# A two-block transformer kernel on one core: order of the linear-attention tail, its norm read out of PSUM, and one wait split in two

## The chip, the cores and the metric

The kernel runs on one core of one Trainium2 chip. The metric is the device time of one execution in microseconds. Before the change the median of three runs was 2160.75 us (2159.34 to 2163.74).

## The reference

Two transformer blocks, one after the other, on 512 tokens of width 1024. The change lies in the first block's gated linear attention (GLA): 4 heads, keys and queries 64 wide, values 128 wide, both directions.

```
q, k, v, g per head; cum = cumsum(g) within a chunk
o_inter = (q * exp(cum)) @ state                       # from the states between chunks
attn    = sum_d q_i k_j exp(cum_i - cum_j), masked     # within a chunk
o       = o_inter + attn @ v                           # both directions added
state   = exp(last) * state + (k * exp(last - cum)).T @ v
out     = rmsnorm(o, gla_norm_g) * silu(r)             # per head, over its 128 columns
mix     = concat([out, diff_attention_out]) @ w_out
x       = x + gate * mix                               # then norm2 and the feed-forward
```

Differential attention (`diff_tensor`, `diff_scalar`, `diff_vector`) runs just before the GLA and gives the other four of the eight 128-row pieces that `w_out` takes.

## The kernel before

Every activation lies transposed, feature on partitions and 512 tokens along the free dimension. A large product is made in three fp32r passes (high weight by high input, high by low, low by high; `three_passes`, L405), so each weight slot of 128 x 1024 is split: ScalarE rounds it to `w_hi` (`split_slots`, L418), GpSimd subtracts to `w_lo` (L1631). Slots come through a ring of four raw buffers, filled by SyncE in stream order; two pairs of split buffers are used by turns. Each engine has one program in a written order, and semaphores tie them. A PSUM bank is taken with `claim` (waits until the last user has freed it) and handed over with `full`.

The GLA is made in chunks of 128 tokens. Keys decayed to the chunk's edge (`key_decay`, `decayed_keys`) are turned (`keys_turned`, L1201 and L1206) and multiplied with the values to the states between chunks (L1228). Between these, TensorE computes the eight chunks `mixed_values_chunk(0..7)` of `w_out` for the differential half (12 matmuls of 512 columns each, 3 passes x 4 pieces). The attention within a chunk is made by levels: level 0 is the diagonal (`gla_level(pe, 0)`, `attention(0)`), and levels 1 to 7 halve the distance each time. For level `li`, VectorE writes four differences of running sums (`sums`, L1389 to L1392: two into `lk`, two into `lq`), ScalarE takes the exponentials of `lk` and `lq` (`level_decay`, L1291), GpSimd multiplies `lk` by the keys (L1429), VectorE `lq` by the queries (L1409), TensorE makes four banks of products (`gla_level`, L1190), banks 0 to 3 for even levels and 4 to 7 for odd, and VectorE (L1376; for levels 1 and 2 ScalarE, L1302) puts them into `attnT`. VectorE's order within turn `li` is: L1409 of `li`, `sums(li + 1)`, `attention(li - 1)`.

Then come the outputs: for each head 4 products of `attnT` with the values (L1247) and 8 of the states with the decayed queries `qe` (L1251) add up in banks 4 to 7. ScalarE copies each output to `og` (L1330) and squares it (L636), TensorE sums the squares over partitions (`head_sum`, L619), ScalarE takes the root (L641), VectorE the reciprocal (L663), TensorE spreads it (`head_spread`, L627), VectorE multiplies it in with the gain (L667) and then with the gate `rT` (L671), ScalarE rounds to `hh` (L652) and VectorE subtracts to `hl` (L657). The first weight slot of the next projection, `mix1`, is split by ScalarE just before it rounds the last head. `half_mixed_tensor` computes the projection, output chunk by output chunk (m = 0 to 7, 12 matmuls each), and `mixed_chunk` (L1488) adds each to the residual.

## Time and profile before

| what | value |
|---|---|
| median of 3 runs | 2160.75 us |
| the profiled execution | 2151.61 us, its span 2149.7 us |
| TensorE matmul busy | 2014.5 us, 94% |
| TensorE weight load busy | 1610.4 us, 75% |
| VectorE, ScalarE, GpSimd busy | 929.1, 739.3, 703.2 us |
| mean granted TensorE clock | 0.961 of full |
| the stretch that the diff touches | about 356 to 487 us of the span |

The profile covers one execution. A slice's or window's PEclk of 1.00 is a TensorE clock of 2.4 GHz, 0.50 is 1.2 GHz. Matmul rows are counted in parts (an fp32 product gives two rows). "Idle before" is the time for which the engine sat still ahead of an instruction, with what it waited for.

### The profile page before, as it was taken

The page shows a single profiled execution, that of the slowest core. Times are in us where ns is not written, and L with a number is a line of the kernel's source. Part 1 is how long each engine was busy: PE and PEld are TensorE (multiplying, and loading weights), DVE is VectorE, ACT ScalarE, POOL GpSimd, SP SyncE. Part 2 cuts the span into 40 slices and gives each one's busy share as a digit, 9 for nine tenths or more (in the row PEclk, how much of TensorE's full clock was granted, in tenths as well). Part 3 has the DMA queues.
Part 4 walks back from the last instruction along what each step waited for, and adds up shares of the span by engine and source line. Part 5 has one row for each costly group of instructions (what it writes and reads, how often), then busy time and mean ns, then how long its engine had stood idle before and what let it go on. Part 6 is the DMA issues. An engine that isn't in the chain of part 4 may idle for free.

```text
span 2149.7 us, 25842 instructions
## 1 busy us (share of the span) xinstructions
PE 2014.5 (94%) x10133; PEld 1610.4 (75%) x10136; DVE 929.1 (43%) x1363; ACT 739.3 (34%) x1202; POOL 703.2 (33%) x296
## 2 busy tenths in 40 slices
PE   5899988879999999999999999889989999999998
PEld 3787856667888888788888877756857777888886
DVE  2622587764344430444443334666775323222102
ACT  3433345433222221422222134536265333222211
POOL 0332100223344444334444423210401433444442
PEclk8999989879999999999999999899989999999999
DMA  8633210002344452334445522200200222232221
GB/s 330 205 130 101 94 56 14 21 11 98 126 142 144 154 195 90 99 125 147 146 151 183 184 70 84 69 30 21 90 29 30 89 79 88 98 98 98 90 96 59
DMA packets 60126, 223.61 MB, mean 104 GB/s; under 512 B 6800, under 2 KB 7056, under 8 KB 58256
## 3 DMA queue, kind: packets, MB, share of 16 engines
q1 hardware_dynamic: 59472, 220.13, 30.1%
q10 hardware_dynamic: 576, 2.43, 0.3%
q8 instruction: 51, 0.84, 0.2%
q14 instruction: 27, 0.22, 0.0%
HBM read 220.43 MB, written 2.10 MB: 104 GB/s over the span
## 4 chain that ended last, share of the span: by engine, by line
PE 85%; DVE 8%; ACT 3%; issue 2%; DMA 1%; SPq 0%; POOL 0%; DVEq 0%; ACTq 0%
PE ps L405 74%; PE ps L537 2%; DMA raw<-stream 1%; DVE t L601 1%; DVE hl L593 1%; PE ps L947 1%; PE ps L2014 1%; PE ps L2167 1%; PE ps L966 1%; DVE neg_max L1104 1%; PE ps L2176 1%; PE ps L1190 0%; ACT w_hi L418 0%; PE ps L2036 0%; DVE step L2297 0%
## 5 line engine op out<-in xcount | busy, mean ns | idle before, releaser
L1631 POOL TENSOR_TENSOR w_lo<-raw,w_hi 128x1024 fp32r<-128x1024 f32 x278 | 670.6, 2413 | 1369.0 <-ACT w_hi L418 765.4
L405 PE MATMUL ps<-hh,w_hi 128*128 128x512 f32 x1528 | 611.1, 400 | 34.3 <-DVE hl L593 17.9
L405 PE MATMUL ps<-hl,w_hi 128*128 128x512 f32 x1528 | 603.4, 395 | 0.0
L405 PE MATMUL ps<-hh,w_lo 128*128 128x512 f32 x1528 | 602.6, 394 | 0.0
L405 PEld LDWEIGHTS ps<-hh,w_hi 128*128 128x128 f32 x1528 | 291.2, 191 | 108.4 <-issue 26.1
L405 PEld LDWEIGHTS ps<-hh,w_lo 128*128 128x128 f32 x1528 | 291.5, 191 | 62.9
L405 PEld LDWEIGHTS ps<-hl,w_hi 128*128 128x128 f32 x1528 | 291.9, 191 | 59.4
L1604 ACT ACTIVATE w_hi<-raw 128x1024 fp32r<-128x1024 f32 x126 | 133.7, 1061 | 472.5 <-PE ps L405 472.5
L464 DVE SCALAR_TENSOR_TENSOR mod_raw<-mod_raw,cond_ada 128x1024 f32<-128x1024 f32 x72 | 116.2, 1615 | 249.7 <-DMA mod_raw<-late 249.7
L405 PE MATMUL ps<-act_hi,w_hi 128*128 (+1 forms) x528 | 209.3, 396 | 0.0
L405 PE MATMUL ps<-act_lo,w_hi 128*128 (+1 forms) x528 | 209.3, 396 | 0.0
L405 PE MATMUL ps<-act_hi,w_lo 128*128 (+1 forms) x528 | 209.3, 396 | 0.0
L1664 DVE TENSOR_TENSOR act_lo<-prod,act_hi 128x512 fp32r<-128x512 f32 x66 | 156.4, 2369 | 57.2 <-ACT act_hi L1609 57.2
L418 ACT ACTIVATE w_hi<-raw 128x1024 fp32r<-128x1024 f32 x92 | 96.9, 1055 | 186.7 <-PE ps L405 183.2
L1623 ACT ACTIVATE w_hi<-raw 128x1024 fp32r<-128x1024 f32 x60 | 63.6, 1061 | 267.6 <-PE ps L405 267.6
L1661 DVE TENSOR_TENSOR prod<-silu,ps 128x512 f32<-128x512 f32 x66 | 45.4, 688 | 216.9 <-PE ps L405 209.0
L405 PEld LDWEIGHTS ps<-act_hi,w_lo 128*128 128x128 f32 x528 | 99.4, 188 | 24.3
L405 PEld LDWEIGHTS ps<-act_lo,w_hi 128*128 128x128 f32 x528 | 99.4, 188 | 24.2
L405 PEld LDWEIGHTS ps<-act_hi,w_hi 128*128 128x128 f32 x528 | 99.4, 188 | 24.2
L464 DVE SCALAR_TENSOR_TENSOR raw<-raw,cond 128x1024 f32<-128x1024 f32 x32 | 47.5, 1499 | 66.5 <-DMA raw<-stream 61.5
L537 PE MATMUL ps<-cst,sq 128*128 128x128 f32 x456 | 63.1, 296 | 10.5 <-ACT sq L556 10.2
L537 PEld LDWEIGHTS ps<-cst,sq 128*128 128x128 f32 x456 | 60.6, 208 | 15.7 <-issue 8.4
(405 smaller groups left out, 2284.8 us busy)
## 6 DMA issues: line engine op xcount, KB each, us to landing
raw<-stream SPq DMA_DIRECT2D x316, 512.0 KB, 3.5
mod_raw<-late SPq DMA_DIRECT2D x72, 512.0 KB, 4.4
mod_w<-mod_w SPq DMA_DIRECT2D x8, 1024.0 KB, 15.6
xT<-xT SPq DMA_DIRECT2D x2, 1024.0 KB, 15.7
xT<-xT ACTq DMA_DIRECT2D x2, 1024.0 KB, 6.1
out<-fin SPq DMA_DIRECT2D x8, 256.0 KB, 2.2
csta<-csta SPq DMA_DIRECT2D x1, 1344.0 KB, 20.4
cT<-cT SPq DMA_DIRECT2D x1, 1024.0 KB, 20.2
```

The lines of the kernel that those rows point to most:

```text
L405: mm = pe.matmul(out, w, r, start=first and i == 0, stop=last and i == 2)
L418: act.activation(halves_of(g)[0][:, :], raw[slot_of[g] % RING][:, :], ACT.Copy).then_inc(S("w_hi_ready"), 1)
L464: dve.scalar_tensor_tensor(out=slot, in0=slot, scalar=1.0, in1=condition, op0=ALU.mult, op1=ALU.mult, accum_out=to)\
L537: mm = pe.matmul(ps[:, ba, t * P:(t + 1) * P], sq[k % 2][:, t * P:(t + 1) * P], c("one").broadcast_to([P, P]), start=(k == 0 and t == 0), ...
L593: dve.scalar_tensor_tensor(out=lo[:, k, :], in0=t1[k % 2][:, 0:tokens], scalar=shift(k), in1=hi[:, k, :].bitcast(F32), op0=ALU.add, op1=AL ...
L601: dve.scalar_tensor_tensor(out=to, in0=src[:, k, :], scalar=gains(k), in1=ps[:, b, 0:tokens], op0=ALU.mult, op1=ALU.mult).then_inc(S("norm ...
L947: mm = pe.matmul(flat[:, r * 1024 + a:r * 1024 + z], dq[rows, h, qt * P:(qt + 1) * P], dk[rows, h, a:z], start=True, stop=True)
L1604: act.activation(w_hi[g % SPLIT][:, :], raw[n % RING][:, :], ACT.Copy).then_inc(S("w_hi_ready"), 1)
L1623: act.activation(w_hi[g % SPLIT][:, :], raw[n % RING][:, :], ACT.Copy).then_inc(S("w_hi_ready"), 1)
L1631: pool.tensor_tensor(lo[:, :], raw[n % RING][:, :], hi[:, :].bitcast(F32), ALU.subtract)\
L1661: dve.tensor_tensor(prod[j][:, :], silu[j][:, :], ps[:, b + 1, :], ALU.mult).then_inc(bank_empty(b + 1), 1)
L1664: dve.tensor_tensor(act_lo[:, at], prod[j][:, :], act_hi[:, at].bitcast(F32), ALU.subtract).then_inc(S("act_ready"), 1)
```

## The change

1. **End of the differential attention.** The last block's product with the values (`mix_values(15)`) now follows `head_squares(0)` directly; `head_squares(1)` to `(3)` follow it. `gla_level(pe, 0)`, all four banks, moves behind the second of the four `head_spread`-like steps (L1215) at the start of `gla_tensor`.
2. **`level_decay`.** The exponential of `lk` waits for the level's first two sums, no longer for all four; that of `lq` waits for all four as before.
3. **Outputs in banks 0 to 3.** `from_states(0)` (state products of heads 0 and 1) is issued ahead of level 7, `from_states(1)` behind it, then `within(h)` adds the `attnT` products head by head.
4. **The norm.** ScalarE squares each output straight from PSUM; VectorE multiplies the output by gain and gate straight from PSUM into `og`; no copy is made. Sums are made for pairs of heads with 2 columns, roots and reciprocals for pairs. The spread factor is multiplied in last.
5. **`mix1`.** Its first two slots are split ahead of the outputs. Its chunks m = 0 and 1 are computed together, piece by piece: piece k waits only for head k; the spreads of heads 2 and 3 are issued behind piece 0.

```diff
-        for h in range(HEADS - 1):
+        head_squares(0)
+        mix_values(len(pairs) - 1)
+        for h in range(1, HEADS):
             head_squares(h)
-        gla_level(pe, 0, (0, 1))
-        mix_values(len(pairs) - 1)
-        gla_level(pe, 0, (2, 3))
-        head_squares(HEADS - 1)
...
         keys_turned(0)
         for h in range(HEADS):
+            if h == 2:
+                gla_level(pe, 0)
...
+        def from_states(pc):
+            for h in (2 * pc, 2 * pc + 1):
+                claim(pe, h, ("og", h))
+            for t in range(NT):
+                for d, at in ((0, t), (1, NT - 1 - t)):
+                    for half in range(2):
+                        rows = slice(64 * half, 64 * half + 64)
+                        pe.matmul(ps[:, 2 * pc + half, t * P:(t + 1) * P], states[rows, d, pc, at, :],
+                                  qe[rows, d, pc * N + t * P:pc * N + (t + 1) * P], start=(t == 0 and d == 0), stop=False,
+                                  skip_group_check=True)
+
+        def within(h):
+            for t in range(NT):
+                mm = pe.matmul(ps[:, h, t * P:(t + 1) * P], vt[:, NTC + t, h * DV:(h + 1) * DV], attnT[:, t, h, :], start=False,
+                               stop=(t == NT - 1), skip_group_check=True)
+            mm.then_inc(bank_full(h), 1)
+
+        def output_sums(pair):
+            claim(pe, 4 + pair, ("ng_ss", pair))
+            for h in (2 * pair, 2 * pair + 1):
+                pe.wait_ge(S("og_squared"), h + 1)
+                for t in range(NT):
+                    at = 2 * ((h % 2) * NT + t)
+                    mm = pe.matmul(ps[:, 4 + pair, at:at + 2], sq[h % 2][:, t * P:(t + 1) * P], c("one").broadcast_to([P, 2]), start=True, stop=True)
+            mm.then_inc(bank_full(4 + pair), 1)
+
         for li in range(1, len(LEVELS) + 1):
+            if li == len(LEVELS):
+                pe.wait_ge(S("qe_ready"), 2)
+                read(pe, ("u", len(directions) - 1, 4))
+                from_states(0)
             pe.wait_ge(S("lq_ready"), li)
             pe.wait_ge(S("lk_ready"), li)
             gla_level(pe, li)
+        from_states(1)
         for b in range(4):
             read(pe, ("level", len(LEVELS), b))
+        within(0)
+        within(1)
+        within(2)
+        output_sums(0)
+        within(3)
+        output_sums(1)
...
         def level_decay(li):
-            act.wait_ge(S("level_sums"), 4 * li)
-            for t, done in ((lk[li % 2], "lk_decay"), (lq[li % 2], "lq_decay")):
+            for sums, t, done in ((2, lk[li % 2], "lk_decay"), (4, lq[li % 2], "lq_decay")):
+                act.wait_ge(S("level_sums"), 4 * (li - 1) + sums)
                 act.activation(t[:, :], t[:, :], ACT.Exp, scale=GATE_SCALE).then_inc(S(done), 1)
...
         roots_ahead(act)
+        split_slots(act, firsts["mix1"] + 1)
+        for pair in range(2):
+            for h in (2 * pair, 2 * pair + 1):
+                b = full(act, ("og", h))
+                if pair:
+                    full(act, ("ng_ss", 0))
+                act.activation(sq[h % 2][:, 0:N], ps[:, b, :], ACT.Square).then_inc(S("og_squared"), 1)
+            if pair == 0:
+                output_root(0)
+        output_high(0)
+        output_high(1)
+        output_root(1)
+        output_high(2)
+        output_high(3)
...
+        def gated_output(h):
+            b = full(dve, ("og", h))
+            dve.wait_ge(S("og_squared"), h + 1)
+            dve.scalar_tensor_tensor(out=og[:, h, :], in0=ps[:, b, :], scalar=v("gla_g"), in1=rT[:, h, :], op0=ALU.mult, op1=ALU.mult)\
+               .then_inc(bank_empty(b), 1)
...
+            dve.tensor_tensor(t1[h % 2][:, 0:N], og[:, h, :], ps[:, b, :], ALU.mult).then_inc(S("og_t"), 1)
...
+        for h in range(2):
+            gated_output(h)
+        output_roots(0)
+        for h in range(2, HEADS):
+            gated_output(h)
+        for pair in range(2):
+            if pair:
+                output_roots(1)
+            for h in (2 * pair, 2 * pair + 1):
+                output_scaled(h)
+            for h in (2 * pair, 2 * pair + 1):
+                output_low(h)
...
+        pe.wait_ge(*spent(slot_of[g0]))
+        output_spread(pe, 0)
+        output_spread(pe, 1)
+        for m in range(2):
+            claim(pe, bank0 + m, (key, m), residual(key, m + 1))
+        for k in range(4):
+            pe.wait_ge(S("og_ready"), k + 1)
+            for m in range(2):
+                mm = three_passes(pe, ps[:, bank0 + m, :], g0, 4 * m + k, P, hh[:, 4 * half + k, :], hl[:, 4 * half + k, :], k == 0, k == 3)
+                if k == 3:
+                    mm.then_inc(bank_full(bank0 + m), 1)
+            if k == 0:
+                output_spread(pe, 2)
+                output_spread(pe, 3)
```

`output_root(pair)` and `output_roots(pair)` take root and reciprocal of the 8 columns of a pair. `output_high(h)` copies `t1` to `hh` on ScalarE, `output_low(h)` subtracts on VectorE and counts `og_ready`. `output_spread(h)` makes 4 transposes into bank 6 or 7 once the pair's reciprocal is there.

## Rows read from the trace of the kernel before

**Rows 1.** The page, busy time by engine.
```profile
PE 2014.5 (94%) x10133; PEld 1610.4 (75%) x10136; DVE 929.1 (43%) x1363; ACT 739.3 (34%) x1202; POOL 703.2 (33%) x296
```
**Rows 2.** The chain that ended last, 350 to 500 us, shares by line.
```profile
by line: PE ps L405 29.2%; issue 7.9%; PE ps L1190 6.8%; DVE attnT L1376 5.7%; PE ps L1228 3.3%; PE ps L1251 3.0%; PE ps L1247 2.8%; ACT attnT L1302 2.5%; PE ps L994 2.4%; PE ps L619 2.2%; PE ps L966 1.9%; DVE lk L1389 1.8%; PE ps L537 1.8%
```
**Rows 3.** TensorE's waits, 355 to 490 us: total, times, longest.
```profile
PE ps L1190 <- DVE lq_odd L1409: 9.6, 3, 4.8
PE ps L1190 <- DVE lq_even L1409: 5.6, 2, 3.6
PE ps L405 <- DVE attnT L1374: 5.2, 1, 5.2
PE ps L405 <- POOL w_lo L1631: 2.6, 1, 2.6
```
**Rows 4.** Timeline, end of differential attention: start, duration, instruction, idle before.
```profile
359.61 2.74 PE L994 MATMUL ps<-cst,squared 128*128 128x2 f32 x24
...
363.92 1.60 PE L966 MATMUL ps<-probT,dvt 128*128 128x128 f32 x12
...
368.26 0.17 DVE L1139 SCALAR_TENSOR_TENSOR std_no<-ps,diff_eps 128x16 f32<-128x16 f32 x1 [7.29 <-PE ps L994]
```
**Rows 5.** Timeline, the spreads and the last low part before the chunks.
```profile
370.57 1.31 PE L1215 MATMUL ps<-cst,rs_no 128*128 128x128 f32 x8 [0.40 <-DVE t L1153]
...
374.13 1.47 DVE L1146 TENSOR_TENSOR hl<-t,hh 128x512 fp32r<-128x512 f32 x2
```
**Rows 6.** Timeline, level 1's sums beside GpSimd's split of the last slot.
```profile
396.52 2.54 POOL L1631 TENSOR_TENSOR w_lo<-raw,w_hi 128x1024 fp32r<-128x1024 f32 x1 [3.06 <-ACT w_hi L418]
396.75 2.85 DVE L1392 TENSOR_TENSOR lq_odd<-cumx 128x512 f32<-128x512 f32 x1
...
401.59 0.60 PE L1201 MATMUL ps<-cst,sq 128*128 128x128 f32 x4
```
**Rows 7.** Timeline, one turn of the level loop, behind the four sums of level 5.
```profile
430.28 2.56 DVE L1376 COPY_PREDICATED attnT<-csta,ps 128x512 f32<-128x512 uint32 x4
430.39 1.06 ACT L1291 ACTIVATE lk<-lk 128x1024 f32<-128x1024 f32 x1 [5.28 <-DVE lq_odd L1392]
...
431.53 2.36 POOL L1429 TENSOR_TENSOR lk<-lk,gkx 128x1024 f32<-128x1024 f32 x1 [4.66 <-ACT lk L1291]
432.74 2.23 DVE L1409 TENSOR_TENSOR lq_odd<-lq_odd,gqx 128x1024 f32<-128x1024 f32 x1
```
**Rows 8.** The chain that ended last, 350 to 500 us, in order of time.
```profile
387.20 2.75 PE ps L405 x12
...
409.34 2.76 PE ps L1190 x32
...
456.45 0.64 PE ps L1247 x4
457.09 0.65 PE ps L1251 x8
```
**Rows 9.** Groups of instructions, 449 to 480 us: busy, mean ns, idle before.
```profile
L667 DVE SCALAR_TENSOR_TENSOR t<-og,vec,ps 128x512 f32<-128x512 f32 x4 | 3.0, 747 | 7.1 <-PE ps L627 7.1
...
L636 ACT ACTIVATE sq<-og 128x512 f32<-128x512 f32 x4 | 2.5, 629 | 0.1
...
L641 ACT ACTIVATE std_ng<-ps,cst 128x4 f32<-128x4 f32 x4 | 1.0, 255 | 0.2 <-PE ps L619 0.2
```
**Rows 10.** Timeline, the tail: level 7, the split before `mix1`, chunk 1's end.
```profile
449.06 4.87 PE L1190 MATMUL ps<-lq_odd,lk 64*128 64x128 f32 x32 [2.92 <-DVE lq_odd L1409]
...
476.60 2.35 POOL L1631 TENSOR_TENSOR w_lo<-raw,w_hi 128x1024 fp32r<-128x1024 f32 x1 [28.67 <-ACT w_hi L418]
...
487.22 0.75 DVE L1488 SCALAR_TENSOR_TENSOR xT<-ps,mod,xT 128x512 f32<-128x512 f32 x1 [2.00 <-PE ps L405]
```
**Rows 11.** Windows: length, busy of PE, PEld, DVE, ACT, POOL, then clock.
```profile
428.00:435.00 7.00, 5.13 (x32) 4.84 (x32) 7.00 (x10) 2.01 (x2) 2.36 (x1) 0.50 0.00 0
...
468.00:479.00 11.00, 3.95 (x30) 3.15 (x29) 8.34 (x13) 5.21 (x11) 2.35 (x1) 0.93 0.00 0
```

More of the change, by code:

```diff
@@ L612, in head_norm_starts @@
         norm_next["rs"] = norm_base[key]["rs"] + HEADS
-    def head_sum(pe, key, h, b):
-        claim(pe, b, (key + "_ss", h))
-        pe.wait_ge(*norm(key, "sq", h + 1))
-        for t in range(NT):
-            mm = pe.matmul(ps[:, b, t * P:(t + 1) * P], sq[h % 2][:, t * P:(t + 1) * P], c("one").broadcast_to([P, P]),
-                           start=True, stop=True)
-        mm.then_inc(bank_full(b), 1)
-    def head_spread(pe, key, h, b):
-        claim(pe, b, (key, h), norm(key, "t1", h + 1))
-        pe.wait_ge(*norm(key, "rs", h + 1))
-        for t in range(NT):
-            mm = pe.transpose(ps[:, b, t * P:(t + 1) * P], rs[key][:, h * NT + t:h * NT + t + 1].broadcast_to([P, P]), ident)
-        mm.then_inc(bank_full(b), 1)
@@ L654, in head_norm_vector @@
-    def head_norm_vector(dve, key, src, chunk0, gains, times, meanwhile=None):
-        def low(h):
-            dve.wait_ge(*norm(key, "hi", h + 1))
-            dve.tensor_tensor(hl[:, chunk0 + h, :], t1[h % 2][:, 0:N], hh[:, chunk0 + h, :].bitcast(F32), ALU.subtract)\
-               .then_inc(S("norm_ready"), 1)
-        for h in range(HEADS):
-            read(dve, (key + "_ss", h))
-            cols = slice(h * NT, (h + 1) * NT)
-            dve.reciprocal(rs[key][:, cols], std[key][:, cols]).then_inc(S("norm_rs"), 1)
-            b = full(dve, (key, h))
-            if h >= 2:
-                dve.wait_ge(*norm(key, "ready", h - 1))
-            dve.scalar_tensor_tensor(out=t1[h % 2][:, 0:N], in0=src[:, h, :], scalar=gains, in1=ps[:, b, :],
-                                     op0=ALU.mult, op1=ALU.mult).then_inc(S("norm_t1"), 1)
-            if times is not None:
-                dve.wait_ge(*norm(key, "t1", h + 1))
-                dve.tensor_tensor(t1[h % 2][:, 0:N], t1[h % 2][:, 0:N], times[:, h, :], ALU.mult)\
-                   .then_inc(S("norm_gated"), 1)
-            if meanwhile is not None:
-                meanwhile(h)
-            if h:
-                low(h - 1)
-        low(HEADS - 1)
@@ L1326, in gla_scalar, with output_high, output_root @@
         roots_ahead(act)
[L1328 to L1333 removed]
+        split_slots(act, firsts["mix1"] + 1)
+        def output_high(h):
+            act.wait_ge(S("og_t"), h + 1)
+            act.activation(hh[:, h, :], t1[h % 2][:, 0:N], ACT.Copy).then_inc(S("og_hi"), 1)
+        def output_root(pair):
+            b = full(act, ("ng_ss", pair))
+            act.activation(std["ng"][:, 2 * NT * pair:2 * NT * (pair + 1)], ps[:, b, 0:4 * NT:2], ACT.Sqrt, bias=c("eps"), scale=1.0 / DV)\
+               .then_inc(bank_empty(b), 1)
[12 more added lines that the diff above has]
+        output_high(3)
     def mix_gate(m):
@@ L1441, in half_slots, with half_mixed_tensor @@
         return ("w_out", [((4 * half + k) * P, P, ((m * P, m * P + P, 0),)) for m in (2 * pair, 2 * pair + 1) for k in range(4)])
-    def half_mixed_tensor(pe, key, half, g0, bank0, ready, sums_of=None):
-        for m in range(KD):
+    def half_mixed_tensor(pe, key, half, g0, bank0, sums_of=None):
+        pe.wait_ge(*spent(slot_of[g0]))
[12 more added lines that the diff above has]
+                output_spread(pe, 3)
+        after[g0] = (bank_full(bank0 + 1), bank_uses[bank0 + 1])
+        for m in range(2, KD):
             g, b = g0 + m // 2, bank0 + m % 4
```

76 lines of the change are left out of this document (20 added, 56 removed).

## The prediction

> **What bounds the kernel now.** I read the page first: TensorE is busy 94% of the span, the next engine 43% [rows 1]. So nearly everywhere only TensorE's own work counts, and a change can gain only where TensorE stands still or runs at half clock. The chain that ended last, cut to 350 to 500 us, shows such a place: next to L405 stand VectorE's and ScalarE's lines and 7.9% of "issue" [rows 2]. TensorE's waits in it name the places [rows 3]: 15.2 us ahead of the levels for VectorE's L1409, 5.2 us ahead of the first `mix1_diff` chunk, 2.6 us for GpSimd's split ahead of `mix1`. I then followed three stretches in the timeline: the end of the differential attention [rows 4, 5], one turn of the level loop [rows 7], and the tail from level 7 to the end of `mix1`'s chunk 1 [rows 8 to 10]. Behind chunk 1 everything is TensorE-bound and unchanged, so the whole effect is how much earlier chunk 1 ends: at 487.2 in the rows [rows 10]. I make the sum as shifts of that moment.
>
> **Part 1, end of the attention.** Now 24 rows of head sums (2.74) and half of level 0 stand ahead of the last value product, which starts at 363.92 [rows 4]; VectorE meanwhile idles 7.29 and continues at 368.26. After the change 8 rows of sums stand ahead (2.74/3 = 0.9), so the product starts at 360.5. Behind it come 24 rows of sums (2.7) in place of half of level 0 and 8 rows. Total ahead of L1139: 0.9 + 1.6 + 2.7 in place of 8.5, so 3.3 less. All of level 0 (32 rows, 2.8 to 3.3) is now between the second and third spread, and nothing hides it in full: the spreads of heads 2 and 3 started at 370.57 [rows 5], with the shift alone 367.3; now they follow level 0, at 370.1. Before, VectorE was busy until 372.0 (the last two low parts at 374.13 less three steps of 0.7, [rows 5]) and only then took the third head, 1.4 behind its spread; now it waits for the spread and takes it 0.65 behind, at 370.8. The low parts that ended at 375.6 [rows 5] end at 374.4. Gain: 1.2. Bounds: 0 if level 0 takes its place in full, 3.3 if VectorE hides it. TensorE's idle there stays 4.7 to 5.2 us [rows 3], so I leave the clock of the first chunk alone.
>
> **Part 2, `lk` waits for its own sums.** In a turn of the loop VectorE is busy 7.00 of 7.00 us [rows 11]. The turn is four sums (0.6 each, 2.4), attention 2.5, and L1409. L1409 shows 2.23, but it starts at 432.74 while GpSimd's product runs until 431.53 + 2.36 = 433.89; what is left behind that is 1.1. So VectorE's two-SBUF product stands still while GpSimd works, 1.1 us a turn, while the attention, which reads PSUM, passes beside GpSimd in its ordinary time [rows 7]. With the change ScalarE starts 1.2 earlier (two sums), GpSimd at 430.33, and ends at 432.69, just ahead of L1409. A turn becomes 5.95. That holds for the turns of levels 5, 6 and 7: 3 x 1.05 = 3.1. In the turn of level 3 it gains 1.0 too (the exponential of `lk` follows ScalarE's level 1 blocks, GpSimd ends 1 earlier); in that of level 4 ScalarE's `qe` exponentials hold it, the 1.0 only persists. TensorE's 5.13 for a level at half clock [rows 11] still fits in 5.95. Gain of the loop: 4.1; bounds 0 (GpSimd gets its start behind a sum and blocks it) to 5.
>
> The same edit has a cost at level 1. There GpSimd still splits the last `mix1_diff` slot, and the fourth sum is held by it: 2.85 in place of some 0.65 [rows 6]. Now `lk`'s exponential is ready long before the split ends at 399.06, and GpSimd goes on to its product directly. The fourth sum slips in (399.0 to 399.6), then GpSimd holds the port for 2.36, to 402.0. Queued on VectorE are the two products of `decayed_keys(3)` (768 columns, by 1.1 for L1409's 1024 some 0.9); they end at 402.9, and TensorE's `keys_turned(3)`, at 401.59 in the rows, waits for them: 1.35 later. VectorE itself is 2.4 late, which its residual and state work pass on to `sums(2)` and L1409 of levels 1 and 2, and the third level's sums start 1.9 later. Cost at that level: 1.9 to 2.0. Bounds: 0 (VectorE's queue wins against GpSimd), and 4.3 if, one step on, GpSimd also gets in ahead of L1409 of level 1, which starts only 0.04 before it by my count. I take 2.0: at 396.7 GpSimd did get in between two VectorE sums [rows 6]. The rule that bears on it is in the Trainium skill, "GPSIMD Engine Reference", the SBUF interfaces row of its first table: they are shared with VectorE, and instructions with two SBUF inputs contend. It names no order and no price, so by it alone the cost might also be 0; the trace shows a full stop.
>
> So L1409 of level 7, over at 449.0 in the rows, is over at 449.0 - 1.2 - 4.1 + 2.0 = 445.7.
>
> **Part 3, states ahead.** `from_states(0)` needs banks 0 and 1 from `attention(6)`, which VectorE does behind L1409 of level 7: two quarters of 2.5 [rows 7] and 0.1, so TensorE starts at 1.35 behind L1409. Queued behind this claim is level 7. Full-clock work in one block: 32 rows of states 2.6 (four times 0.65, [rows 8]), level 7 2.76, `from_states(1)` 2.6: 8.0. The loop before ran at half clock (0.50, [rows 11]), and level 7 was at half clock for most of its 4.87 [rows 10]; I add 2.1, half of some 4.2 us. `attention(7)` (VectorE) is hidden under `from_states(1)`: bank 3 is in `attnT` 0.8 after level 7, the states take 2.6. The `attnT` products start at 445.7 + 1.35 + 8.0 + 2.1 = 457.1, later than before, but with all state products done. Bounds: 455.0 if the clock is up, 458 if it stays down longer.
>
> **Part 4, the norm.** Let W be this start. A head's product is 8 rows of L1247, 1.28 [rows 8]. Three heads: W + 3.85. Squares of heads 0 and 1 (0.63, [rows 9]) end at 3.3, hidden. Sums of a pair, 16 rows at 0.114 [rows 4]: 1.8, to 5.65. Head 3: 6.95. The sums of pair 1 wait for head 3's square only at their second half: 6.95 to 8.75. Spreads of heads 0, 1 (0.65 each, [rows 5]): result at 9.4 and 9.95. VectorE's `output_scaled` (0.75, as L667 [rows 9]): 10.15 and 10.8; `output_high(0)` (0.63) 10.8; `output_low(0)` (0.7, [rows 5]) behind the second `output_scaled`: 11.5, and `output_low(1)` 12.1. The second pair's root (0.26, [rows 9]) stands behind `output_high(1)` on ScalarE, its reciprocal behind `output_low(1)`: 12.35. TensorE takes piece 0 at 11.55 (6 matmuls at 2.75/12 = 0.23, [rows 8]: 1.4), then spreads 2 and 3 to 14.1, pieces 1 to 3 at 14.1, 15.75 and 17.15, and ends chunks 0 and 1 at 18.6. Reading PSUM twice instead of copying costs no more by rows of the same shape: L667 reads one PSUM operand in 0.75, the square takes 0.63 from SBUF [rows 9], between 0.6 and 0.75 from PSUM. `mix1`'s first slots are split in ScalarE's gap after its last exponentials, under `attention(6)` and `(7)`, which read PSUM; the split that TensorE waited for until 478.95 [rows 10] is gone from the path, and so is GpSimd's hold on VectorE's gate product.
>
> Chunk 1 ends at 457.1 + 18.6 = 475.7 instead of 487.1 (VectorE's row starts 0.1 behind it, [rows 10]). **Sum: 11.4 us**: 1.2 + 4.1 - 2.0 + 8.1 for the tail (449.0 to 487.1 is 38.1, 445.7 to 475.7 is 30.0). The profiled execution took 2151.61, with 1.9 outside its span, and would take 2140.2. It lies 9.1 under the median of the runs shown; the difference carries over, so 2160.75 - 11.4 = 2149.3. About 0.2%, 4.3 us, is what a measurement of this kernel can tell from no change.
>
> **Rivals.**
> - *GpSimd wins twice.* L1409 of level 1 also waits: another 2.3, sum 9.1, time 2151.7. For it: a margin of 0.04. Against: VectorE's instruction is issued first. Chance 0.2.
> - *No collision.* The port goes to VectorE's queue: 13.4, 2147.3. Against it the 2.85 row [rows 6]. Chance 0.17.
> - *The split wait gives nothing.* If GpSimd starts in front of the third and fourth sum and stops them, each turn keeps its 7.0, and 4.1 is lost: 7.3, 2153.5. Against: the fourth sum starts 0.65 before GpSimd. Chance 0.1.
> - *Slower: the clock of the tail.* The norm becomes bursts with pauses on TensorE. If the clock falls at W and stays at 1.2 GHz to the end of chunk 1, rows that take 2.76 at full clock take 5.13 at half [rows 8, 11], 1.86 times. Of the tail's work, 24 chunk matmuls 5.5, products 5.1, sums 3.6, spreads 2.6, 8.0 of states and level 7 less 2.1 counted: 22.7 x 0.86 = 19.5 more, time 2168.8. It decides from some 11.4/19.5 = 58% of the tail at half clock on. Against: before, 11 us with TensorE busy only 3.95 kept a clock of 0.93 [rows 11], and the new tail has no pause as long. Chance 0.04. This is the Trainium skill's "TensorE: Matmul & The Clock Gate", "HAM oscillation": pauses between bursts make the chip halve the clock, so a sparser tail would be paid for twice. By the rows the loop at 5.13 of 7.0 busy ran at half and the sparser norm at nearly full [rows 11], so the busy share alone doesn't decide it here.
>
> **How the numbers follow.** The forecast with its own small errors (clock at `from_states`, +-2, and the pieces at the end, +-1.5) has 0.49. Cases together reach from 2147 to 2154; the median of a few runs moves by 2 either way (2159.3 to 2163.7). Range 2143.5 to 2155.5. Every case but the clock's gains over 4.3 us by itself; where two of the losing cases meet (another 2.3 and 4.1 lost, 5.0 left) and the median moves by 2, or the clock falls for half of the tail, the result is within 0.2%: 0.06. Slower: 0.03, most of the clock rival. Faster: 0.91.
>
> **What the profile after would show.** Level turns of 6.0 with the L1409 of levels 5 to 7 at 1.2 and not 2.2; around level 1, the two `decayed_keys` products held some 2 us by GpSimd's first `lk` product, and a pause of 1.3 ahead of `keys_turned(3)`; L1139 3.3 earlier but the first chunk only 1.2 earlier; no wait of L405 on GpSimd at `mix1`; chunk 1 some 30 us behind level 7's L1409. The prediction is wrong if turns stay at 7.0, if the pause at level 1 exceeds 3, or if PEclk reads 0.50 behind the `attnT` products.

## The result, and the profile after

The kernel after the change takes 2141.03 us, median of 7 runs (2133.14 to 2143.61). The kernel before has a median of 2152.29 over 7 runs (2147.85 to 2163.74): the three known ones and four more beside the changed kernel, all four between 2147.85 and 2152.29. The ratio is 0.9932, 95% interval 0.9907 to 0.9956. On 2152.3 that is a gain of 14.6 us (9.5 to 20.0); the two medians differ by 11.3. The change is faster, by somewhere about the 11.4 us of the sum or more, yet the time is 8.3 below the forecast 2149.3 and outside the range 2143.5 to 2155.5. What failed is above all the time that the sum was subtracted from.

Where the two profiled executions part, in stages, each from one row of the timeline to the next (us; "predicted" is the prediction's own sum, stage by stage):

| stage | before | predicted | after |
|---|---|---|---|
| start of L1139/L1070 (`std_no`) | 368.26 | 365.0 | 364.73 |
| from there to the first `mix1_diff` chunk | 8.9 | 11.0 | 14.2 |
| to the fourth `keys_turned` | 24.5 | 25.8 | 25.9 |
| to the end of level 7's `lq` product | 47.4 | 44.0 | 43.8 |
| to the end of chunk 1 of `mix1` | 38.2 | 30.0 | 30.0 |
| end of chunk 1 | 487.2 | 475.7 | 478.6 |
| from there to the end of the span | 1662.5 | unchanged | 1663.1 |

The last three stages ahead of chunk 1 are as predicted within 0.2 us; the one to the first `mix1_diff` chunk is 3.2 longer. The end of a chunk is here the start of VectorE's row on it. In the changed kernel the rows of chunks 0 and 1 are printed as one, "x2", and that of chunk 1 starts 0.7 behind the time printed. Lines are renumbered: L994 is now L927, L966 is L899, L1190 is L1121, L1201 is L1132, L1291 is L1245, L1376 is L1348, L1392 is L1364, L1409 is L1381, L1429 is L1435, L1631 is L1650, L1247 is L1179, L1251 is L1173, L1146 is L1077, L1488 is L1507, and L1215, the spreads of the differential attention, is L1148. L1215 of the new kernel is `output_spread`.

The end of the attention, timeline of after, against [rows 4, 5]:

```profile
361.52 3.10 PE L927 MATMUL ps<-cst,squared 128*128 128x2 f32 x24
...
364.73 0.17 DVE L1070 SCALAR_TENSOR_TENSOR std_no<-ps,diff_eps 128x16 f32<-128x16 f32 x1 [4.10 <-PE ps L927]
...
367.64 5.13 PE L1121 MATMUL ps<-gqx,gkx 64*128 64x128 f32 x32
...
372.70 1.97 PE L1148 MATMUL ps<-cst,rs_no 128*128 128x128 f32 x8
...
378.97 0.77 PE L405 MATMUL ps<-hh,w_hi 128*128 128x512 f32 x1 [4.30 <-issue]
```

`std_no` is 3.5 earlier, 3.3 were counted. But level 0 takes 5.13 us for its 32 rows, between the second and the third spread, and the spreads 1.97 for 8 rows where 1.31 stood. The window shows the clock (columns as in [rows 11]), in after and then in another execution of the same kernel:

```profile
364.00:372.00 8.00, 8.00 (x47) 7.67 (x48) 2.52 (x5) 2.35 (x5) 0.00 (x0) 0.50 0.00 1
440.00:448.00 8.00, 5.13 (x32) 4.84 (x32) 8.00 (x13) 4.11 (x6) 3.73 (x2) 0.64 0.00 1
```

```profile
364.00:372.00 8.00, 7.03 (x55) 6.34 (x55) 3.88 (x7) 2.93 (x6) 0.00 (x0) 0.79 0.00 1
```

In `after` TensorE was granted 0.50, 1.2 GHz, from 364 to 372, though it was busy all 8 us. In the second execution the clock fell at the same place, but was up again at 367.3, ahead of nearly all of level 0: the window shows 0.79, and the first chunk began 2.7 us sooner behind `std_no`.

Level 1, timeline of after, against [rows 6]:

```profile
398.78 2.87 DVE L1364 TENSOR_TENSOR lq_odd<-cumx 128x512 f32<-128x512 f32 x1
...
401.06 2.85 POOL L1435 TENSOR_TENSOR lk<-lk,gkx 128x1024 f32<-128x1024 f32 x1
...
401.56 2.62 DVE L1014 TENSOR_TENSOR sq<-sq,gkc 128x256 f32<-128x256 f32 x1
...
404.84 0.66 PE L1132 MATMUL ps<-cst,sq 128*128 128x128 f32 x4 [1.08 <-DVE sq L1015]
...
410.29 1.22 DVE L1381 TENSOR_TENSOR lq_odd<-lq_odd,gqx 128x1024 f32<-128x1024 f32 x1
410.34 3.40 POOL L1435 TENSOR_TENSOR lk<-lk,gkx 128x1024 f32<-128x1024 f32 x1 [6.43 <-ACT lk L1245]
```

One turn of the loop, timeline of after, against [rows 7]:

```profile
431.86 1.06 ACT L1245 ACTIVATE lk<-lk 128x1024 f32<-128x1024 f32 x1 [4.07 <-DVE lk L1362]
...
432.95 2.56 DVE L1348 COPY_PREDICATED attnT<-csta,ps 128x512 f32<-128x512 uint32 x4
432.99 2.37 POOL L1435 TENSOR_TENSOR lk<-lk,gkx 128x1024 f32<-128x1024 f32 x1 [3.46 <-ACT lk L1245]
...
435.40 1.22 DVE L1381 TENSOR_TENSOR lq_odd<-lq_odd,gqx 128x1024 f32<-128x1024 f32 x1
```

At 398.78 a sum stands 2.87 us for the split, at 401.56 the first product of `decayed_keys(3)` stands 2.62 for GpSimd's `lk` product, and TensorE waits 1.08 for it. L1381 of level 1 keeps its 1.22, and now it is GpSimd that takes 3.40: of the race that the prediction saw 0.04 apart, VectorE won. From level 5 on ScalarE starts 1.2 sooner, GpSimd is over at 435.36 (432.99 + 2.37), and L1381 takes 1.22 where 2.23 stood. The waits of TensorE from 355 to 480 us (total, times, longest), against [rows 3]:

```profile
PE ps L1121 <- DVE lq_even L1381: 7.6, 3, 3.9
PE ps L405 <- issue: 4.3, 1, 4.3
PE ps L1121 <- DVE lq_odd L1381: 4.0, 2, 3.0
PE ps L1173 <- DVE attnT L1348: 2.2, 1, 2.2
...
PE ps L1132 <- DVE sq L1015: 1.1, 1, 1.1
```

15.2 us ahead of the levels have become 11.6, with 2.2 more ahead of the states, now for `attention(6)`, and no wait on GpSimd is left. The second of the windows shown first, 440 to 448, has the clock at 0.64, just ahead of the states, and their 32 rows take 3.79 where 2.6 was counted at full clock.

The tail, timeline of after, against [rows 8 to 10]:

```profile
447.35 1.25 DVE L1381 TENSOR_TENSOR lq_odd<-lq_odd,gqx 128x1024 f32<-128x1024 f32 x1
...
450.00 3.79 PE L1173 MATMUL ps<-qe,states 64*128 64x128 f32 x32 [2.21 <-DVE attnT L1348]
...
453.55 3.46 PE L1121 MATMUL ps<-lq_odd,lk 64*128 64x128 f32 x29
...
459.06 2.94 PE L1179 MATMUL ps<-attnT,vt 128*128 128x128 f32 x24
...
461.84 1.84 PE L1189 MATMUL ps<-cst,sq 128*128 128x2 f32 x16
...
466.65 1.95 PE L1215 MATMUL ps<-cst,rs_ng 128*128 128x128 f32 x8
...
470.07 0.77 PE L405 MATMUL ps<-hh,w_hi 128*128 128x512 f32 x1 [1.47 <-DVE hl L1416]
...
472.77 1.14 PE L1215 MATMUL ps<-cst,rs_ng 128*128 128x128 f32 x8
...
478.00 1.43 DVE L1507 SCALAR_TENSOR_TENSOR xT<-ps,mod,xT 128x512 f32<-128x512 f32 x2 [1.81 <-PE ps L405]
```

TensorE enters the states 1.4 us behind L1381's end, is in the `attnT` products 10.5 behind it (predicted 11.4), goes from them to the end of chunk 1 in 19.6 (predicted 18.6), and the total is the predicted 30.0 because the two misses cancel.

The part behind the `attnT` products was counted at full clock. Two windows show where it was not, first in `after`, then in the kernel before:

```profile
466.60:473.40 6.80, 5.33 (x20) 4.29 (x21) 2.78 (x5) 1.42 (x3) 0.00 (x0) 0.53 0.00 0
```

```profile
479.00:484.30 5.30, 5.30 (x13) 4.15 (x14) 1.79 (x3) 1.58 (x2) 2.37 (x1) 0.50 0.33 99
```

In `after` the clock stood at half over the first two spreads (1.95 for 8 rows, 1.14 for the next 8 at full clock) and over piece 0, whose six matmuls took 2.70 us instead of 1.4: some 2.1 us more. In `before` it stood at half over all of chunk 0 of `mix1`, whose 12 matmuls took 5.3 us where chunk 1's took 2.75: some 2.5 more. Such a stretch of half clock stands there in all four profiles of each kernel, so both tails pay about the same for it.

### The profile page after: what moved, and what is told of

The parts are those of the page before. It is cut to its first block, busy times and chain, and to the rows that moved or that the text cites. A ratio compares the mean times of both kernels' runs of the same rounds, so it can differ in the third digit from the quotient of the medians.

```text
span 2141.7 us, 25860 instructions
## 1 busy us (share of the span) xinstructions
PE 2011.9 (94%) x10133; PEld 1611.4 (75%) x10136; DVE 926.4 (43%) x1361; ACT 737.7 (34%) x1196; POOL 703.8 (33%) x296
## 3 DMA queue, kind: packets, MB, share of 16 engines
q1 hardware_dynamic: 59472, 220.13, 30.1%
## 4 chain that ended last, share of the span: by engine, by line
PE 84%; DVE 9%; ACT 3%; issue 2%; DMA 1%; SPq 0%; POOL 0%; DVEq 0%; ACTq 0%
PE ps L405 72%; PE ps L537 2%; DVE hl L593 1%; DVE t L601 1%; DMA raw<-stream 1%; DVE neg_max L1035 1%; PE ps L2033 1%; PE ps L880 1%; PE ps L2186 1%; PE ps L2195 1%; PE ps L899 1%; DVE step L2316 0%; PE ps L2055 0%; PE ps L2207 0%; PE ps L817 0%
## 5 line engine op out<-in xcount | busy, mean ns | idle before, releaser
L1650 POOL TENSOR_TENSOR w_lo<-raw,w_hi 128x1024 fp32r<-128x1024 f32 x278 | 669.8, 2410 | 1364.5 <-ACT w_hi L418 760.7
L405 PEld LDWEIGHTS ps<-act_lo,w_hi 128*128 128x128 f32 x528 | 99.4, 188 | 24.2
L405 PEld LDWEIGHTS ps<-act_hi,w_hi 128*128 128x128 f32 x528 | 99.4, 188 | 24.2
L464 DVE SCALAR_TENSOR_TENSOR raw<-raw,cond 128x1024 f32<-128x1024 f32 x32 | 47.4, 1495 | 66.3 <-DMA raw<-stream 61.3
L537 PE MATMUL ps<-cst,sq 128*128 128x128 f32 x456 | 62.9, 295 | 10.6 <-ACT sq L556 10.2
```

The source lines that it names most:

```text
L405: mm = pe.matmul(out, w, r, start=first and i == 0, stop=last and i == 2)
L464: dve.scalar_tensor_tensor(out=slot, in0=slot, scalar=1.0, in1=condition, op0=ALU.mult, op1=ALU.mult, accum_out=to)\
L537: mm = pe.matmul(ps[:, ba, t * P:(t + 1) * P], sq[k % 2][:, t * P:(t + 1) * P], c("one").broadcast_to([P, P]), start=(k == 0 and t == 0), ...
L1650: pool.tensor_tensor(lo[:, :], raw[n % RING][:, :], hi[:, :].bitcast(F32), ALU.subtract)\
```

## The experiments

Each kernel was timed against the kernel before on the same chip. The stages named are those of the table; "tail" is the last one before the span's rest.

**1. The kernel before again**, nothing edited.

> The kernel before, unchanged, timed against itself, to see how far its own median moves. Theory (the effect was about as forecast and the level to which it was applied was off): ratio within 0.2% of 1.000 with a median of its own near 2152, some 8 us under the 2160.75 that the forecast started from. Rival (2160.75 is its usual time and the later runs were the exception): median 2159 to 2164.

Measured: ratio 1.0007 (0.9991 to 1.0023). The median is 2154.03, and that of the 17 runs beside it 2152.78. Seven of its twelve runs lie at 2151.0 to 2154.8, five at 2158.8 to 2162.6. Over the 67 runs of this kernel that were timed for the experiments the times go from 2143.8 to 2162.9 without a clear gap: 46 lie under 2155, 6 between 2155 and 2158, 15 above. So these are no two separate groups; but the three runs that the prediction knew (2159.34 to 2163.74) lie all among the slowest quarter, its profiled execution (2151.61) in the middle, and their median stood some 8 us over what the kernel mostly takes. The mean granted clock goes with the time: 0.954 to 0.960 in the 15 runs above 2158, 0.960 to 0.967 in the 46 under 2155. The mean time times the mean clock is nearly the same for both, 2160.7 x 0.9575 = 2069 and 2151.2 x 0.9626 = 2071, so by this estimate the clock is enough to account for the spread. Why one execution is granted less than another stays open.

**2. The kernel after again**, nothing edited.

> The changed kernel, unchanged, for a second profile and ratio. Theory A (the half clock over level 0 and the spreads was no accident but comes with the new order of TensorE's work): the clock again falls before level 0, level 0 takes about 5 us instead of 2.8, and the first chunk starts some 14 us behind the mean of the squares (the line that writes std_no). Theory B (accident): level 0 at 2.8 us, first chunk 11 us behind it. Ratio 0.993 to 0.996 under either; 0.1% between them.

Measured: 0.9919 (0.9902 to 0.9937), 2137.3 us. That is a gain of 17.4 us (13.6 to 21.1), and 11.4 lies outside it. `std_no` to the first chunk takes 11.5 us, so Theory B holds; the predicted 11.0 is nearly met once level 0 runs at full clock (2.88 for 32 rows).

**3. Level 0 behind all four spreads.**

```diff
-            if h == 2:
-                gla_level(pe, 0)
...
+        gla_level(pe, 0)
         for i, (d, pc) in enumerate(directions):
```

> Changed kernel, with all of level 0 behind the four spreads instead of between the second and third. Theory (level 0 between the spreads delays the low parts of heads 2 and 3, and the time in which TensorE waits for them would have held it): the first chunk starts 8.9 us behind the line that writes std_no, as in the kernel before, 5 us less than in the changed kernel's profile if the clock is at half there and 2 less if it is full; ratio to before 0.001 to 0.0025 lower than the changed kernel's. Rival (attention(0) then waits for level 0, nothing is won): the distance stays at 11 to 14 us, ratio as the changed kernel's.

Measured: 0.9906 (0.9886 to 0.9926), first stage 9.48 us. Its timeline:

```profile
364.54 3.40 PE L1146 MATMUL ps<-cst,rs_no 128*128 128x128 f32 x16
...
367.88 2.82 PE L1121 MATMUL ps<-gqx,gkx 64*128 64x128 f32 x32
...
373.07 0.47 PE L405 MATMUL ps<-hh,w_hi 128*128 128x512 f32 x1 [2.37 <-issue]
```

The 16 rows of spreads run together, level 0 fills the pause ahead of the chunk (from 4.72 to 2.37), and 2.0 us of the 2.65 that the change paid there come back. In time it is not to be told from experiment 2.

**4. The end of the attention as before**, all else changed.

```diff
-        head_squares(0)
+        for h in range(HEADS - 1):
+            head_squares(h)
+        gla_level(pe, 0, (0, 1))
         mix_values(len(pairs) - 1)
-        for h in range(1, HEADS):
-            head_squares(h)
+        gla_level(pe, 0, (2, 3))
+        head_squares(HEADS - 1)
...
-            if h == 2:
-                gla_level(pe, 0)
```

> Changed kernel, with the end of the differential attention and level 0 in their old order. Theory A (the new order gave away more than it won, because of the half clock): 2 us faster than the changed kernel, first chunk 8.9 us behind the line that writes std_no, that line 3.4 later. Theory B (the forecast's 1.2 us gain holds where the clock doesn't fall): 1.2 us slower than the changed kernel.

Measured: 0.9916 (0.9897 to 0.9936), first stage 8.88 as before, but `std_no` at 371.61, 3.3 later than before. Of these, 1.8 stood already ahead of the first squares (361.37 against 359.61), and the rest comes from half clock behind them: the last value product took 2.78 where 1.60 stood. The times of 2 and 4 overlap, so part 1 is worth less than a measurement of this kernel can tell. By the rows: `std_no` 3.5 sooner, the stage behind 2.65 longer, gain 0.9.

**5. `lk` waits for all four sums again.**

```diff
-            for sums, t, done in ((2, lk[li % 2], "lk_decay"), (4, lq[li % 2], "lq_decay")):
+            for sums, t, done in ((4, lk[li % 2], "lk_decay"), (4, lq[li % 2], "lq_decay")):
```

> Changed kernel, with the exponential of lk waiting for all four sums again. Theory: turns of levels 5 to 7 return from 6.0 to 7.0 us, level 3's from 5.8 to 7.6, and the pause at level 1 goes (the fourth keys_turned 24.5 us behind the first chunk's start instead of 25.9); net 2.2 us slower than the changed kernel, ratio to before some 0.001 higher. Rival (GpSimd's lock on VectorE isn't what the turn gains from, the product of lq is): turns stay at 6.0.

Measured: 0.9943 (0.9921 to 0.9965). The loop stage is back at 47.40 from 43.7, the stage around level 1 falls from 25.9 to 24.6. Its timeline shows one turn as it was:

```profile
434.13 1.06 ACT L1245 ACTIVATE lk<-lk 128x1024 f32<-128x1024 f32 x1 [5.28 <-DVE lq_odd L1364]
...
435.26 2.36 POOL L1435 TENSOR_TENSOR lk<-lk,gkx 128x1024 f32<-128x1024 f32 x1 [4.65 <-ACT lk L1245]
436.47 2.24 DVE L1381 TENSOR_TENSOR lq_odd<-lq_odd,gqx 128x1024 f32<-128x1024 f32 x1
```

Turns of 7.0 and L1381 at 2.24 return. 3.7 gained in the loop and 1.3 lost at level 1 are the change's share: 2.4 net, predicted 2.1. The rival fell.

**6. `lk` of level 1 alone waits for all four.**

```diff
-            for sums, t, done in ((2, lk[li % 2], "lk_decay"), (4, lq[li % 2], "lq_decay")):
+            for sums, t, done in ((4 if li == 1 else 2, lk[li % 2], "lk_decay"), (4, lq[li % 2], "lq_decay")):
```

> Changed kernel, with level 1 alone waiting for all four sums. Theory (at level 1 GpSimd's product goes in ahead of decayed_keys(3)): that product of VectorE falls from 2.6 to 0.4 us, no pause ahead of the fourth keys_turned, 24.5 us behind the first chunk's start instead of 25.9, turns of 6.0 kept; 1.4 us off at level 7 at the least, up to 3 as VectorE's own queue is 2.4 earlier. Rival (the pause has another cause, such as the split of the last slot): 25.9 stays.

Measured: 0.9918 (0.9895 to 0.9941). Around level 1 24.69, the loop 43.38: both halves of the gain at once. Its timeline:

```profile
398.31 0.41 DVE L1014 TENSOR_TENSOR sq<-sq,gkc 128x256 f32<-128x256 f32 x1
...
399.56 2.39 POOL L1435 TENSOR_TENSOR lk<-lk,gkx 128x1024 f32<-128x1024 f32 x1 [1.73 <-ACT lk L1245]
...
400.36 0.60 PE L1132 MATMUL ps<-cst,sq 128*128 128x128 f32 x4
```

The `decayed_keys` product takes 0.41 in place of 2.62 and TensorE's `keys_turned` waits for nobody. So the early start of this one `lk` product made the collision; the rival fell, for the split of the slot is the same in both.

**7. States of heads 0 and 1 behind level 7**, their waits with them.

```diff
-            if li == len(LEVELS):
-                pe.wait_ge(S("qe_ready"), 2)
-                read(pe, ("u", len(directions) - 1, 4))
-                from_states(0)
...
+        pe.wait_ge(S("qe_ready"), 2)
+        read(pe, ("u", len(directions) - 1, 4))
+        from_states(0)
         from_states(1)
```

> Changed kernel, with from_states(0) behind level 7, next to from_states(1). Theory (the states ahead of level 7 only make level 7 wait for attention(6), as attention(7) is hidden under from_states(1) anyway): from level 7's lq product to the first attnT product 9.1 us instead of 10.5, 1.3 faster. Rival (the states ahead fill an idle stretch of TensorE and so win their 2.6 us): 2 to 4 us slower, 12 to 13 in place of 10.5.

Measured: 0.9922 (0.9898 to 0.9945); tail 29.1. Its timeline:

```profile
444.29 4.26 PE L1121 MATMUL ps<-lq_odd,lk 64*128 64x128 f32 x29 [0.86 <-DVE lq_odd L1380]
...
448.72 3.74 PE L1173 MATMUL ps<-qe,states 64*128 64x128 f32 x61
```

TensorE starts 0.1 behind L1380's end instead of 1.4, because level 7 need not wait for `attention(6)`, and the `attnT` products follow 8.15 us behind L1380's end instead of 10.5. Putting the states ahead of level 7 therefore hides nothing: it costs 2.3 us up to the `attnT` products. By the whole tail it costs only 0.9, because in this execution half clock lay over more of the work behind them (458.4 to 468.6, 10.2 us; in `after` 6.8). In time the edit is inside the spread of experiment 2.

**8. The kernel before with one split earlier**, the slot that TensorE waited for.

```diff
         roots_ahead(act)
+        split_slots(act, firsts["mix1"])
```

> Kernel before, with the first slot of mix1 split right behind the roots that ScalarE loads ahead, and nothing else. Theory: no wait of TensorE on GpSimd at mix1, VectorE's last gate product 0.7 instead of 2.3 us; mix1 starts at 27.4 us behind level 7's lq product in place of 30.0, and the sum 2.0 to 2.6 us, ratio 0.9990. Rival (TensorE then waits for the heads one by one and nothing is won): m = 0 ends as before, ratio 1.000.

Measured: 0.9974 (0.9956 to 0.9991), a gain of 5.6 us (1.9 to 9.5) from one line. The theory's 2.0 to 2.6 is inside the interval, at its low end. From head 3's spread to chunk 0's end 4.6 us pass instead of 8.7. The wait of 2.63 on GpSimd is gone, and VectorE's gate product takes 0.69; but the 12 matmuls of chunk 0 also ran at full clock here (1.00 from 485.0 to 489.3), where they had run at half, which is worth 2.5 by the window of `before`, while 0.8 of new waiting for a head came in. So the 4.1 us won there are the wait and the clock together; whether the clock stays up because TensorE no longer stands still ahead of them is not shown by one profile. Ahead of it the states ran for 14 us at 0.50, and the tail is 41.2, so for the whole gain the time speaks here, not that profile.

**9. Experiments 3, 6 and 7 together.**

> Changed kernel with level 0 behind the spreads, level 1 alone waiting for all four sums, and from_states(0) behind level 7. Theory (the three costs are separate and add): first chunk 9.5 us behind the line that writes std_no, fourth keys_turned 24.5 to 25 behind that, the first attnT product 8.2 to 9.3 behind level 7's lq product; 2.0 + 2.0 + 1.3 = 5 us less than the changed kernel, ratio to before 0.9895. Rival (one wait takes the other's place): 2 us less at the most, 0.991.

Measured: 2130.25 (2123.73 to 2132.32, 6 runs), 0.9893 (0.9869 to 0.9918). All its runs lie below the lowest of experiment 2 (2132.47). Stages: 9.4, 23.8, 43.4, 26.0; chunk 1 ends at 466.6. The tail is 2.5 shorter than any other's. Its `attnT` products start 6.4 behind level 7's `lq` product, where 8.15 (experiment 7) and 10.5 stood; behind them it takes the same 19.6 as `after`. The window, and the timeline behind level 7's product:

```profile
440.00:448.00 8.00, 7.30 (x104) 7.18 (x105) 5.60 (x9) 1.56 (x2) 4.72 (x2) 1.00 0.41 129
```

```profile
440.70 2.48 PE L1121 MATMUL ps<-lq_odd,lk 64*128 64x128 f32 x29 [1.11 <-DVE lq_odd L1379]
...
443.35 3.74 PE L1172 MATMUL ps<-qe,states 64*128 64x128 f32 x61
...
465.96 1.43 DVE L1505 SCALAR_TENSOR_TENSOR xT<-ps,mod,xT 128x512 f32<-128x512 f32 x2 [1.98 <-PE ps L405]
```

Here the clock is 1.00 from 440 to 448, where after had 0.64, and level 7 takes 2.48 for its 29 rows where 3.46 or 4.26 stood: the step from 8.15 to 6.4 is the clock's. From `std_no` to chunk 1 it is 8.7 us shorter than experiment 2, against the 5 that were forecast; in time the gain is 7 by the medians and 5.6 by the ratios.

**10. The split late again**, behind the roots of the second pair; TensorE's wait for the slot moves behind the first two spreads, so that it waits where it did before.

```diff
         roots_ahead(act)
-        split_slots(act, firsts["mix1"] + 1)
...
         output_root(1)
+        split_slots(act, firsts["mix1"])
         output_high(2)
         output_high(3)
+        split_slots(act, firsts["mix1"] + 1)
```

> Changed kernel, with mix1's slots split as late as before: the first on ScalarE behind the second root, the second behind the last hh. Theory: piece 0 waits for GpSimd's 2.35 us, some 3.5 us later than in the changed kernel (470.1 there, 21.5 behind level 7's lq product), mix1's chunks 0 and 1 end 33.5 instead of 30 behind it; ratio 0.0015 above the changed kernel's. Rival (heads 2 and 3 then set the end): 1 us at the most.

Measured: 2142.63, 0.9948 (0.993 to 0.9965); tail 33.5 against 30.0. Its timeline:

```profile
466.24 2.34 POOL L1651 TENSOR_TENSOR w_lo<-raw,w_hi 128x1024 fp32r<-128x1024 f32 x1 [23.80 <-ACT w_hi L418]
...
468.64 0.80 PE L405 MATMUL ps<-hh,w_hi 128*128 128x512 f32 x1 [4.96 <-POOL w_lo L1651]
...
476.58 1.43 DVE L1508 SCALAR_TENSOR_TENSOR xT<-ps,mod,xT 128x512 f32<-128x512 f32 x2 [1.83 <-PE ps L405]
```

TensorE waits 4.96 for GpSimd and takes piece 0 3.5 later behind level 7's `lq` product; from there on both kernels take 8.6, with piece 0 at half clock in both. The early split is worth 3.5 us, the largest single part of the tail's 8, and the rival fell.

**11. The output copied out of PSUM as before**: ScalarE copies each head into `og` and squares the copy; VectorE gates the copy in place.

```diff
+                act.activation(og[:, h, :], ps[:, b, :], ACT.Copy).then_inc(bank_empty(b), 1)
+                read(act, ("og", h))
-                act.activation(sq[h % 2][:, 0:N], ps[:, b, :], ACT.Square).then_inc(S("og_squared"), 1)
+                act.activation(sq[h % 2][:, 0:N], og[:, h, :], ACT.Square).then_inc(S("og_squared"), 1)
```

> Changed kernel, with each output copied by ScalarE to SBUF first, the square and the gated product read from the copy. Theory (the copies lie under TensorE's products except head 3's): 0.4 to 0.6 us later at chunk 1, nothing to see in the ratio. Rival (reading PSUM directly is a main part of the gain): 2 us or more, one copy of 0.6 for each head on the path.

Measured: 0.992 (0.9893 to 0.9948); tail 32.0. Its timeline:

```profile
460.89 0.59 ACT L1298 ACTIVATE og<-ps 128x512 f32<-128x512 f32 x1
...
462.29 2.92 PE L1189 MATMUL ps<-cst,sq 128*128 128x2 f32 x16 [0.60 <-ACT sq L1300]
...
471.19 1.91 PE L1215 MATMUL ps<-cst,rs_ng 128*128 128x128 f32 x8
```

The copy (0.59) puts each square one instruction back, TensorE waits 0.60 for it, and the spreads of heads 2 and 3 fall into 1.91 us of half clock (463.1 to 473.4 at 0.50, 10.2 us against 6.8 in `after`). 1.9 in this execution, of which the longer half clock is the larger part by this count; in time not to be told from experiment 2.

**12. The chunks one after the other**, not in pairs.

```diff
-        for k in range(4):
-            pe.wait_ge(S("og_ready"), k + 1)
-            for m in range(2):
+        for m in range(2):
+            for k in range(4):
+                pe.wait_ge(S("og_ready"), k + 1)
```

> Changed kernel, with chunks 0 and 1 of mix1 one after the other again (heads 2 and 3 still spread behind the first piece). Theory: pieces of 3 matmuls (0.7 us) leave TensorE waiting for the heads, piece 3 is at the earliest where it is now, and all 12 matmuls of chunk 1 (2.75) follow: chunk 1 ends 2 us later than in the changed kernel, chunk 0 0.5 earlier. Rival (the chunks are bound by the spreads of heads 2 and 3 alone, which come 0.7 to 1.3 earlier here): within 1 us.

Measured: 0.9923 (0.9898 to 0.9948); tail 30.5. Its timeline:

```profile
473.11 0.75 DVE L1507 SCALAR_TENSOR_TENSOR xT<-ps,mod,xT 128x512 f32<-128x512 f32 x1 [1.06 <-PE ps L405]
...
475.84 0.75 DVE L1507 SCALAR_TENSOR_TENSOR xT<-ps,mod,xT 128x512 f32<-128x512 f32 x1 [1.98 <-PE ps L405]
```

Chunk 0 now ends 2.7 ahead of chunk 1, chunk 1 0.4 later than with pairs. The order of the matmuls is worth 0.4, and the rival held: the spreads of heads 2 and 3 start 22.9 behind level 7's `lq` product instead of 24.2, and only one wait for a head, 0.76, comes in.

**13 to 16. Two more executions of each kernel**, profiled, nothing edited.

> Another profile of the kernel before. Theory (the stretch behind chunk 1, whose instructions are the same in both kernels, takes some 4 us less in the changed kernel because the clock falls less often there): 1662 to 1670 us behind chunk 1's end. Rival (chance, the same spread in both): somewhere in 1655 to 1670, as likely low as high.

> Another profile of the changed kernel. Theory: 1655 to 1660 us behind chunk 1's end. Rival: 1655 to 1670, as likely high as low. Under both: chunk 1 ends 30.0 us behind level 7's lq product, first chunk 11.5 or 14.2 behind the line that writes std_no, by the clock.

> As the first further look at the kernel before: theory 1662 to 1670 us behind chunk 1's end, rival anywhere in 1655 to 1670.

> As the first further look at the changed kernel: theory 1655 to 1660 us behind chunk 1's end, rival anywhere in 1655 to 1670.

Measured, before: 2150.14 and 2152.56; after: 2132.43 and 2142.32. With the first two profiles of each:

| | tail | end of chunk 1 | from there to the end |
|---|---|---|---|
| before, 4 profiles | 38.2, 38.2, 40.1, 44.4 | 487.2, 486.6, 490.3, 492.0 | 1662.5, 1662.5, 1657.9, 1658.6 |
| after, 4 profiles | 30.0, 30.1, 28.5, 30.2 | 478.6, 475.4, 472.3, 477.4 | 1663.1, 1659.9, 1658.2, 1663.0 |

Chunk 1 ends at 489.0 on the mean before and at 475.9 after, 13.1 sooner: level 7's `lq` product ends 2.6 sooner (3.3 predicted), and the tail is 10.5 shorter (8.1 predicted). Behind chunk 1 both kernels show the same 1658 to 1663, 1660.4 against 1661.1 on the mean, so the theory of a gain there fell. In `before` the tail is long where the clock is low: 11.3, 11.4, 19.0 and 27.3 us of its four tails ran at half clock, of those of `after` 14.1, 14.1, 11.1 and 14.3. The window of the longest tail of before, 448 to 470:

```profile
448.00:470.00 22.00, 20.72 (x121) 17.91 (x121) 4.98 (x9) 2.61 (x5) 0.00 (x0) 0.54 0.00 1
```

Its clock is 0.54 where TensorE is busy 20.7 of 22 us.

## Why the prediction was right in its parts and wrong in its time

- **The failed step** is the last one, from the sum to the time: "It lies 9.1 under the median of the runs shown; the difference carries over, so 2160.75 - 11.4 = 2149.3", with "the median of a few runs moves by 2 either way". The 9.1 was no constant between a profiled and a timed run. By experiment 1 this kernel's times spread over 19 us with the granted clock, and three runs had all fallen among the slowest quarter. Measured with more runs before has medians of 2151.7 to 2154.0; 2152.3 less the same 11.4 is 2140.9, and 2141.03 was measured. The profiled execution's own time, which the prediction had turned down, gave 2140.2. The term for how far a median moves should have been 8, as two known times of one kernel, 2151.61 and 2160.75, already showed.
- **The sum itself** came near in size, in part by luck. Between the first two profiles chunk 1 ends 8.6 us sooner (487.2 to 478.6), not 11.4, since part 1 lost 1.8 there instead of winning 1.2; in the tail two misses of opposite sign cancel. The tail of `before` that the sum started from was the shortest of four: on the mean of four profiles each the gain at chunk 1 is 13.1, and the repeat of the timing (experiment 2) puts the whole gain at 13.6 to 21.1, above 11.4. So that 2152.3 - 11.4 falls on 2141.03 within 0.2 is chance.
- **Part 1 (1.2 predicted).** 0.9 by the rows at full clock (experiments 2 to 4). In `after` itself level 0 fell into half clock and the part lost 1.8. Of the nine other profiled executions with this front, one (experiment 5) shows the same 14.2 us and the rest 10.4 to 11.7, so the long form is a matter of the execution, not of the edit; leaving the clock alone was right for most executions and not for this profile.
- **Part 2, the loop (4.1).** 3.7 measured by undoing it (experiment 5), turns 6.0, L1381 1.22. Right.
- **Part 2, the collision (-2.0).** Right in place and kind: the held product 2.62, TensorE's wait 1.08 (1.35 predicted). Undoing it at level 1 alone returned 1.2 there and 0.3 in the loop, 1.5. The rival in which GpSimd wins twice fell: L1381 of level 1 took 1.22. The rival without a collision fell too. So did the one in which turns stay at 7.0.
- **Part 3 (states ahead).** W came 10.5 behind L1381 against 11.4 counted. What the prediction did not weigh was the other order: experiment 7 shows that putting them ahead costs 2.3 us up to the `attnT` products and 0.9 by the tail of its one profile, since level 7 then waits for `attention(6)` with them.
- **Part 4 (the norm).** From the `attnT` products to chunk 1's end 19.6 against 18.6 counted. The sum had the clock at full throughout, and it was at half for 6.8 us, over two spreads and piece 0, for some 2.1 us more; the rest came out 1.1 shorter than counted. Undone one by one: the early split 3.5, no copy up to 1.9 with the clock in it, pairs 0.4. Two reads of PSUM cost nothing to see: the square took 0.60 from PSUM, VectorE's gated product some 0.8 (1.64 for two). That the split wait was a main thing lay in the prediction's text (2.6 of wait and the hold on the gate product); experiment 10 shows it with the clock the same, experiment 8 by the time.
- **The clock rival (slower).** Its time fell, but its sign came: PEclk reads 0.50 behind the `attnT` products, from 466.1 to 473.0, which the prediction had named as a sign of being wrong. It was 6.8 of 19.6 us and not all of them, and the kernel before paid nearly as much at the same place. The argument against the rival, a clock of 0.93 from 468 to 479 in `before`, stopped too early: that window ends just as the clock falls (477.4), and chunk 0 behind it ran at 0.50. Over the executions it is the tail of *before* that varies (38.2 to 44.4) with its time at half clock, while that of after stays at 28.5 to 30.2. That spread of *before*'s tail is why its mean gain is 10.5 in place of 8.1. The true gain is not known closer than by the two intervals, 9.5 to 20.0 and 13.6 to 21.1.

## What to carry to other kernels

Make the sum from one profiled execution and subtract it from that execution's own time; where three timed runs all lie 8 us off it, widen the range to hold both, and compare the mean granted clocks, for the times of this one kernel spread over 19 us with them. A clock read over a window is a mean: see what it is in the rows right behind the window too. A wait of TensorE that stands behind a whole engine's queue is found by undoing one line: here one weight split issued earlier was worth 3.5 us of a change of some 12 to 17. After each edit look at what the freed engine starts next; GpSimd's product, started 1.2 sooner, ran into VectorE's next two-input product, and holding it back at that one level gave the time back.
